# A two-layer fp32 transformer kernel: the MLP's down product as seven block products per quarter, with the result by tokens

## The reference

```python
        h2 = rmsnorm(x, pre_norm_mlp[l])
        y = jnp.square(jax.nn.relu(h2 @ w_up[l])) @ w_down[l]
        x = x + rmsnorm(y, post_norm_mlp[l])
    return x
```

## Time and profile before

| | |
|---|---|
| three runs, median (lowest to highest) | 953.04 us (952.84 to 953.87) |
| profiled execution, its span | 951.7 us |
| TensorE busy, matmuls | 943.3 us, 99%, 5234 records |
| VectorE busy | 587.3 us, 62% |
| ScalarE busy | 417.5 us, 44% |
| GpSimd busy | 100.4 us, 11% |
| DMA | 89 GB/s over the span |

### The profile page before, as it was taken

The page is one execution under the profiler, slowest core; times in us unless marked ns, Lnnn a source line. Parts: engine busy times, 40 slices in busy tenths (PEclk is TensorE's granted clock), DMA queues, the critical chain, the costliest instruction groups (busy, mean ns, idle before and its releaser), DMA issues.

```text
span 951.7 us, 13474 instructions
## 1 busy us (share of the span) xinstructions
PE 943.3 (99%) x5234; PEld 774.8 (81%) x5234; DVE 587.3 (62%) x1062; ACT 417.5 (44%) x773; POOL 100.4 (11%) x109
## 2 busy tenths in 40 slices
PE   9999999999999999999999999999999999999998
PEld 7779777778898777777778889988888888888887
DVE  6668759898658788765656625863244344445545
ACT  6465346455645456444553234562342233212332
POOL 2004204321220000000002212000000000000021
PEclk9999999999999999999999999999999999999999
DMA  7322121122325112121222442353233322323102
GB/s 246 110 69 67 46 67 67 46 67 78 113 70 196 60 64 67 53 72 38 86 67 89 127 161 70 121 187 113 89 108 92 108 89 89 110 89 92 42 1 89
DMA packets 25918, 85.99 MB, mean 90 GB/s; under 512 B 2944, under 2 KB 5952, under 8 KB 25600
## 3 DMA queue, kind: packets, MB, share of 16 engines
q1 hardware_dynamic: 25040, 80.45, 26.1%
q10 hardware_dynamic: 576, 4.36, 1.2%
q0 software_dynamic: 240, 0.33, 0.1%
HBM read 80.93 MB, written 4.19 MB: 89 GB/s over the span
## 4 chain that ended last, share of the span: by engine, by line
PE 86%; DVE 8%; ACT 2%; issue 1%; DMA 1%; SPq 0%; DVEq 0%; ACTq 0%
PE PB L418 13%; PE PB L420 13%; PE PB L419 13%; PE PB L1010 5%; PE PB L1008 5%; PE PB L1009 5%; PE PB L648 4%; PE PB L685 3%; PE PB L663 2%; DVE wl L1504 2%; PE PB L888 2%; PE PB L890 2%; PE PB L889 2%; PE PB L459 2%; PE PB L463 2%; PE PB L458 2%
## 5 line engine op out<-in xcount | busy, mean ns | idle before, releaser
L418 PE MATMUL PB<-hh,wh 128*128 128x512 f32 x576 | 235.2, 408 | 0.0
L420 PE MATMUL PB<-hh,wl 128*128 128x512 f32 x576 | 224.8, 390 | 0.0
L419 PE MATMUL PB<-hl,wh 128*128 128x512 f32 x576 | 224.6, 390 | 0.0
L1504 DVE TENSOR_TENSOR wl<-raw,wh 128x1024 fp32r<-128x1024 f32 (+2 forms) x90 | 113.7, 1263 | 50.9 <-ACT wh L1048 50.5
L418 PEld LDWEIGHTS PB<-hh,wh 128*128 128x128 f32 x576 | 108.2, 188 | 28.2 <-issue 6.4
L420 PEld LDWEIGHTS PB<-hh,wl 128*128 128x128 f32 x576 | 108.1, 188 | 23.3
L419 PEld LDWEIGHTS PB<-hl,wh 128*128 128x128 f32 x576 | 108.3, 188 | 23.0 <-issue 2.2
L1048 ACT ACTIVATE wh<-raw 128x1024 fp32r<-128x1024 f32 (+2 forms) x90 | 91.3, 1018 | 53.4 <-PE PB L463 14.0
L1215 ACT ACTIVATE S<-S,sm 128x256 f32<-128x256 f32 (+3 forms) x96 | 50.6, 528 | 105.0 <-DVE sm L1607 80.8
L1504 DVE TENSOR_TENSOR wl<-AR,wh 128x1024 fp32r<-128x1024 f32 x55 | 67.6, 1230 | 40.4 <-ACT wh L1048 40.4
L1048 ACT ACTIVATE wh<-AR 128x1024 fp32r<-128x1024 f32 x55 | 57.8, 1052 | 71.0 <-PE PB L1010 71.0
(11 more groups left out here) (380 smaller groups left out, 1688.4 us busy)
## 6 DMA issues: line engine op xcount, KB each, us to landing
AR<-in_dne SPq DMA_DIRECT2D x32, 512.0 KB, 3.6
AR<-in_upe SPq DMA_DIRECT2D x24, 512.0 KB, 3.5
raw<-in_w2g SPq DMA_DIRECT2D x16, 512.0 KB, 3.4
raw<-in_w1e SPq DMA_DIRECT2D x10, 512.0 KB, 3.4
raw<-in_w1q SPq DMA_DIRECT2D x8, 512.0 KB, 3.4
raw<-in_woab SPq DMA_DIRECT2D x8, 512.0 KB, 3.5
raw<-in_w2e SPq DMA_DIRECT2D x5, 512.0 KB, 4.5
raw<-in_w1c SPq DMA_DIRECT2D x4, 512.0 KB, 3.4
```

Source lines behind the costliest of these rows:

```text
L418: e.matmul(bank[:], a[:, col(k)], xa[:, k, :], start=k == 0, stop=False)
L419: e.matmul(bank[:], a[:, col(k)], xb[:, k, :], start=False, stop=False)
L420: i = e.matmul(bank[:], b[:, col(k)], xa[:, k, :], start=False, stop=k == 7)
L1504: e.tensor_tensor(low_, raw_of(c), high.bitcast(F32), ALU.subtract).then_inc(*up("lo", c))
```

## The change

The down product of a quarter is (512 tokens x 1024 hidden) by (1024 x 1024). Tokens, hidden and output features are each cut in two, and the eight products of blocks are replaced by seven products of sums and differences of blocks (`PRODUCTS`): four block sums on each side, and the seven results are combined into four. On the hidden side `bh`, `bl` hold high and low of the plain blocks, `th`, `tl` those of four mixed ones (`hidden`, `mixed`). On the weight side slots a, b, c, d hold blocks (two chunks each): `third` writes a - c into c, `second` d - that into d, `fourth` b - that into b, all on VectorE, and a += d is the accumulating DMA that GpSimd issues. A product is two pieces of 12 matmuls. Features are now the stationary operand and weights stream, so results are token by feature, two banks per product, `2 * (n % 3) + s`.

Up tiles only have banks 6 and 7 (`tenant(6 + m % 2, ...)`); banks 4 and 5 are also `TT`, into which VectorE writes the mixed hidden blocks. The products are summed over the quarters in SBUF (`PS`), with the combination folded into the last quarter's sums (`added`). The sum for the second norm is four matmuls of one column (`sums(2, 7)`) ahead of the last product of quarter 0. The result by tokens needs X by tokens: 32 transposes by TensorE (`turned_x`), 16 ahead of the last product and 16 behind it. GpSimd multiplies by the gain, ScalarE squares and sums, VectorE adds the residual (`final`), and the store is by tokens. The tiles by halves of 256 tokens are gone.

```diff
-        s += [("dne", 8 * q + i, NW) for i in range(8)]
+        s += [("dn", 14 * q + i, NW) for i in range(14)]
...
+PRODUCTS = (("b", 0, "a"), ("b", 1, "b"), ("t", 1, "d"), ("t", 0, "a"), ("t", 2, "c"), ("b", 2, "b"), ("t", 3, "d"))
+SUMMED = {2: "s2", 4: "s3", 5: "s4"}
...
+        PS = [[ar(1024 * n + 512 * s, 512) for s in range(2)] for n in range(4)]
+        PS += [[ar(12288 + 1024 * n + 512 * s, 512) for s in range(2)] for n in range(2)] + [[acc[:], R[:]]]
+        SQ2, TT = PS[5], [PB[4], PB[5]]
+        th, tl = (x[:, :, :].rearrange("p (j i) t -> p j (i t)", i=2) for x in (gh, gl))
...
+            def features(n, j, s):
+
+                kind, i = PRODUCTS[n][0:2]
+                w = slice((256 * i + 128 * s), (256 * i + 128 * s) + 128)
+                return (bh[:, j, w], bl[:, j, w]) if kind == "b" else (th[:, j, w], tl[:, j, w])
...
+            def turned_x(b, at):
+
+                for h in range(2):
+                    bank, before = tenant(at + h, "fin", b, h)
+                    e.wait_ge(*to(*before))
+                    for k in range(4):
+                        i = e.transpose(bank[:, col(k)], X[:, 4 * h + k, col(b)], ident)
+                    i.then_inc(*up("xt", b, h))
+
...
+                    bank, before = tenant(6 + m % 2, "re", q, m)
+                    tile(upper(q, m), bank, before, hh, hl)
+                for n in range(7):
+                    got = [tenant(2 * (n % 3) + s, *summed(q, n, s)) for s in range(2)]
+                    if (q, n) == (0, 6):
                         e.wait_ge(*to("xs", 2, 7))
-                        total(2, 6)
-                    half(c, 4, bank, hh, hl)
...
+                        sums(2, 7)
+                    if n == 2:
+                        e.wait_ge(*to("tw", q, 3, 1))
+                    e.wait_ge(*to("lo", piece(q, n, 0)))
+                    if (q, n) == (3, 6):
+                        turned_x(2, 6)
+                        turned_x(3, 2)
+                        e.wait_ge(*to("lo", piece(q, n, 1)))
+                        for s in range(2):
+                            bank, before = got[s]
...
+                            x.then_inc(*up("gemm", "last", s))
+                        turned_x(0, 4)
+                        turned_x(1, 6)
+                        break
+                    for j in range(4):
+                        c = piece(q, n, j // 2)
+                        a, b, w = wh[c % 3], wl[c % 3], slice(512 * (j % 2), 512 * (j % 2) + 512)
+                        if j == 2:
+                            e.wait_ge(*to("lo", c))
+                        if n < 2:
+                            e.wait_ge(*to("bl", q, j, n))
+                        for s in range(2):
+                            bank, before = got[s]
+                            if j == 0:
+                                e.wait_ge(*to(*before))
...
+                            x = e.matmul(bank[:], high, b[:, w], start=False, stop=j == 3)
+                        if j % 2:
+                            x.then_inc(*up("gemm", c))
...
+                    if n == 3:
+                        e.wait_ge(semaphore(f"sum_a{jj}"), 16 * q + 16)
+                    elif n in SUMMED:
+                        e.wait_ge(*to("sc", q, SUMMED[n], jj))
+                    else:
+                        e.wait_ge(*arrived(PRODUCTS[n][2], jj, q, n == 6))
...
-                    e.wait_ge(*to("gemm", c - 3 if c < LAST else CH["upe", 27]))
-                e.activation(wide_high if c == LAST else wh[c % 3][:, 0:PLAN[c][2]], raw_of(c), ACT.Copy).then_inc(*up("hi", c))
+                    e.wait_ge(*to("gemm", c - 3))
+                e.activation(wh[c % 3][:, 0:PLAN[c][2]], raw_of(c), ACT.Copy).then_inc(*up("hi", c))
...
+                e.wait_ge(*to("gemm", upper(q, m)))
...
+                    e.wait_ge(*to("bl", *((q, j - 2) if m > 3 else (q - 1, j + 2)), 1))
+                e.activation(u, seat["re", q, m][:], ACT.Relu).then_inc(*up("re", q, m))
...
+                e.activation(u, u, ACT.Square).then_inc(*up("uq", q, m))
+                e.wait_ge(*to("uq", q, m))
+                if m % 2:
+                    e.activation(bh[:, j, 256:768], u, ACT.Copy).then_inc(*up("uh", q, j, 1))
+                else:
+                    e.activation(bh[:, j, 0:256], u[:, 0:256], ACT.Copy).then_inc(*up("uh", q, j, 0))
...
+            def mixed(q, j):
+
+                e.wait_ge(*to("tc", q, j))
+                for x in range(2):
+                    e.activation(th[:, j, 512 * x:512 * x + 512], TT[x][:], ACT.Copy).then_inc(*up("th", q, j, x))
...
+            def hidden(q, m):
+
+                j, b = m // 2, tmp[m % 4]
+                if m % 2 == 0:
+                    e.wait_ge(*to("uh", q, j, 0))
+                    e.tensor_tensor(bl[:, j, 0:256], b[:, 0:256], bh[:, j, 0:256].bitcast(F32),
+                                    ALU.subtract).then_inc(*up("bl", q, j, 0))
+                    return
+                a, t = tmp[m % 4 - 1], [TT[i // 2][:, 256 * (i % 2):256 * (i % 2) + 256] for i in range(4)]
+                e.wait_ge(*to("uq", q, m))
...
+                e.tensor_tensor(t[0], a[:, 256:512], a[:, 0:256], ALU.subtract).then_inc(*up("tc0", q, j, 0))
+                e.tensor_tensor(t[2], b[:, 256:512], a[:, 256:512], ALU.subtract).then_inc(*up("tc0", q, j, 2))
+                e.wait_ge(*to("tc0", q, j, 0))
+                e.tensor_tensor(t[1], b[:, 256:512], t[0], ALU.subtract).then_inc(*up("tc0", q, j, 1))
+                e.wait_ge(*to("tc0", q, j, 1))
+                e.tensor_tensor(t[3], b[:, 0:256], t[1], ALU.subtract).then_inc(*up("tc", q, j))
+                e.wait_ge(*to("uh", q, j, 1))
+                e.tensor_tensor(bl[:, j, 256:768], b[:], bh[:, j, 256:768].bitcast(F32),
+                                ALU.subtract).then_inc(*up("bl", q, j, 1))
...
+            def mixed(q, j):
+
+                for x in range(2):
+                    t = slice(512 * x, 512 * x + 512)
+                    e.wait_ge(*to("th", q, j, x))
+                    e.tensor_tensor(tl[:, j, t], TT[x][:], th[:, j, t].bitcast(F32), ALU.subtract).then_inc(*up("tw", q, j, x))
...
+                e.tensor_tensor(slot("c", jj), slot("a", jj), slot("c", jj), ALU.subtract).then_inc(*up("sc", q, "s3", jj))
...
+                e.tensor_tensor(slot("d", jj), slot("d", jj), slot("c", jj), ALU.subtract).then_inc(*up("sc", q, "s2", jj))
...
+                e.tensor_tensor(slot("b", jj), slot("b", jj), slot("d", jj), ALU.subtract).then_inc(*up("sc", q, "s4", jj))
...
+                if q < 3:
+                    e.wait_ge(*to(*summed(q - 1, n, s)))
+                    sum_to(PS[n][s], bank, "ye", q, n, s)
+                    return
...
+                if n == 0:
+                    e.wait_ge(*to("yv", 2, 1, s))
+                    sum_to(PS[1][s], bank, "yv", 3, 0, s)
+                    e.wait_ge(*to("yv", 2, 2, s))
+                    sum_to(PS[2][s], bank, "ye", 3, 0, s)
...
+            def final(b, h):
+
+                t = slice(512 * h, 512 * h + 512)
+                e.wait_ge(*(to("yg1") if (b, h) == (1, 1) else to("yg", b, h)))
+                e.wait_ge(*to("tf", b))
+                e.wait_ge(*to("xt", b, h))
+                e.scalar_tensor_tensor(YG[b][:, t], YG[b][:, t], FAC[:, b:b + 1], seat["fin", b, h][:],
+                                       ALU.mult, ALU.add).then_inc(*up("fin", b, h))
...
+                        lo(upper(q, m) + 2)
+                    if q and m < 2:
+                        added(q - 1, 6, m)
+                    if m % 2 == 0 and m > (4 if q == 0 else 0):
+                        mixed(q, m // 2 - 1)
+                    n = m - (4 if q == 0 else 2)
+                    if n in (0, 1):
+                        third(q, n)
...
                     if (q, m) == (1, 1):
                         root(2)
-                    squared(q, m)
...
+                        e.tensor_tensor(acc[:], acc[:], SQ2[k % 2], ALU.add).then_inc(*up("xs", 2, k))
+                    c = CH["dn", 14 * q + n] + 2
+                    if c < len(PLAN):
+                        lo(c)
+                    if n == 1:
+                        mixed(q, 3)
+                    if n in (2, 4):
+                        fourth(q, n // 2 - 1)
+            added(3, 6, 0)
+            for b in (2, 3):
+                for h in (1, 0):
+                    final(b, h)
+            added(3, 6, 1)
+            final(0, 0)
+            final(0, 1)
+            e.wait_ge(*to("ye", 3, 6, 1))
+            e.wait_ge(semaphore("postg"), 16)
+            e.tensor_tensor(YG[1][:, 512:1024], result(1, 1), POSTG[:, 512:1024], ALU.mult).then_inc(*up("yg1"))
+            final(1, 0)
...
-            for m in range(1, 4):
-                added_y(3, m)
-            for x in range(2):
-                t = half_of[x]
-                for m in (4, 5, 6, 7)[:4 - x]:
-                    e.wait_ge(*to("yq", 3, m, x))
```

(41 more changed lines are left out.)

423 lines of the change are left out of this document (200 added, 223 removed), and 14 rows, old and new, of the table SIGNALS.

## The result

The changed kernel takes **945.67 us** in the median of four runs (944.15 to 947.49), the kernel before 952.96 (952.84 to 953.87): a ratio of 0.9922, 95% interval 0.9908 to 0.9936. It is faster, by 7.3 us, where 16.7 were forecast; the range of 930.5 to 944.5 misses it by 1.2. Run again on another chip it took 944.9 (ratio 0.9911, interval 0.9896 to 0.9926).

The account below looks back on a forecast made before the run. TensorE, busy 99% of the span, was taken as the bound: 951.7 - 23.5 + 1.9 + 1.9 + 4.3 + 0.3 + 0.8 + 0.4 - 2.8 = 935.0 us of span, 936.3 with 1.3 for the median; range 930.5 to 944.5.

Parts of the forecast that it names:

- tiles by halves gone: Down product: its last four tiles' 192 half-width matmuls, with one matmul of ones among them, go from TensorE, -23.5 us.
- 16 transposes ahead of the last product: TensorE: 16 of the 32 transposes of X come before the last product, about 0.115 us each, +1.9 us.
- waits at (0,6) and (1,1): Up tiles: (0,6) waits for the Relu of (0,4), +1.9 us; (1,1) waits for root(2) to free bank 7, +4.3.
- restart, and half clock behind three waits: TensorE behind the two up-tile waits: a restart of a step or so, +0.3 us; no half clock in the sum.
- VectorE late in the last down stage, GpSimd beside it: Last down stage: VectorE's 35.3 us against TensorE's 34.5, +0.8; two GpSimd gain products slowing VectorE by 0.25 each, +0.4.
- sum in bank 7, small steps: TensorE: the second norm's sum becomes four one-column matmuls instead of two records of 512 columns, cost 0.
- the end: After the last wide matmul: eleven VectorE instructions, then a store of 2.65 us; 7.1 us instead of 9.9, -2.8.
- the rival on the clock: TensorE's granted clock falls to its lower level behind the 4.3 us wait: 938 to 942 us, chance 0.05.
- VectorE bounds the last quarter: Last quarter: VectorE's instructions 10% dearer, adding 3 to 4 us there and 1 elsewhere: 939.5 to 944.5 us, chance 0.17.
- The first 672 matmuls of the down product: Down stage: seven products, 672 matmuls over four quarters, cost as before although features are loaded and weights stream, 0.
- The accumulating DMA was covered: Each quarter: slot a += slot d takes 8.4 us, at most 15.5, with 15 to 19.6 us of cover, cost 0.
- The rivals that let it decide: Accumulating DMA outlasts its cover, so piece 6's high part waits: 944 to 951 us, chance 0.03; slower than 953, 0.06.

Follow-up runs that it names:

- The kernel before with the wait alone: The kernel before with its ones matmul total(2) moved to the bank that up tile (1,1) takes, so that tile waits for root(2): 960.19 us against 953.18.
- the four banks: The changed kernel with up tiles taking banks 6, 7, 2 and 3 in turn instead of 6 and 7 alone: 936.68 us, ratio 0.9824.
- the late gain: The changed kernel with GpSimd's products with the gain started only behind VectorE's last low part: 940.39 us, ratio 0.9862.
- with root(2) first: The changed kernel with root(2) on VectorE ahead of the low parts of tiles (1,3) and (1,0), bank 7 still shared: 938.24 us, ratio 0.9842.
- the kernel with the weight sum on VectorE: The changed kernel with slot a += slot d made by VectorE instead of GpSimd's accumulating DMA: 944.95 us, ratio 0.9909.
- unedited: The changed kernel run again without any edit, as the measure for the experiments on the other chip: 944.9 us, ratio 0.9911.
- the last four kernels: The changed kernel with four banks and late gain products (932.28 us); also quarter 0's second weight sum later (931.03); that with a += d on VectorE (933.3), or last store split (930.84).

## Why the prediction was wrong, point by point

The direction, the places and most sizes held; the sum failed by 9.4 us, for two of its terms and two smaller ones. In the profiles' spans, the forecast's terms, and what the profile after shows:

| term | forecast | measured |
|---|---|---|
| tiles by halves gone | -23.5 | -23.5 |
| 16 transposes ahead of the last product | +1.9 | +2.0 |
| waits at (0,6) and (1,1) | +6.2 | 1.8 + 4.2, with their gaps +6.3 |
| restart, and half clock behind three waits | +0.3 | +0.3 and +4.8 |
| VectorE late in the last down stage, GpSimd beside it | +1.2 | 0.8 + 0.7 + 2.2 = +3.7 |
| sum in bank 7, small steps | 0 | +0.9 |
| the end | -2.8 | -1.9 |
| opening of this one profile | 0 | +1.8 |
| sum (span 951.7) | 935.0 | 946.2 (rows add to 946.1) |

**The failed step is the clock.** The forecast put 0.3 behind the two waits and made the fall of the clock a rival of 0.05, though it had found the wait of 4.2 that sets it off, and had seen that nothing in the kernel before could speak for a full clock behind such a wait, since its longest was 1.1. The Trainium skill ("TensorE: Matmul & The Clock Gate", "HAM oscillation — how this bites in real kernels") says that kernels whose TensorE idles for a few us pay with a throttled stretch; the trace agrees, for 4.2 us, and shows the same behind waits of 1.8 and 2.2, shorter than the 3 to 5 of the page's example. That the trace before showed no such fall was no evidence against it. The kernel before with the wait alone, and the four banks, settle the cause from both sides: 7.0 us for a wait of 4.6, and 8.2 off the median (10.1 off the profiled span, where the third stretch stayed away too) where waits of 6.0 went and one of 1.1 came. By itself this step would have made the forecast 941.1, inside the 938 to 942 of the rival on the clock; it took the next one and the small rows of the table to leave the range.

**The second is GpSimd beside VectorE.** The text read 0.25 us per product off one pair of rows and took it for the price. There GpSimd's instruction (909.09, 1.30 us) ended 0.4 us after VectorE's began (909.99). So the two overlapped for 0.4 us only, and VectorE's record ended 1.08 behind GpSimd's, as the low parts of the new stage do. In the new stage overlaps of 0.79, 1.24, 1.23 and 1.20 us cost VectorE 0.65, 1.09, 1.10 and 1.07: in all five places the loss is the overlap less some 0.15. The small price was that of a short overlap. The rule of the Trainium skill ("SBUF — State Buffer", "Who interferes with whom"), that the two block each other for a whole instruction, was weighed and set aside for that row, which is no evidence against it. The page also says that a VectorE instruction with one SBUF input at most is left alone (outside its two-port modes), and the sums from PSUM agree (675 to 692 ns). The trace after bears the rule out (3.9 us on VectorE, 2.5 of them on TensorE), and the late gain shows that this was the cause. The rival "VectorE bounds the last quarter" had the right engine, with a price of 10% on all its instructions; the price was on four of them.

**The end.** Eleven instructions in a row, as worked out, but a final took 0.66, not 0.605, and the last store, of 256 KB where the row's was of 128, 3.15 to the end, not 2.65: 0.9.

**What held.** The first 672 matmuls of the down product cost as before, with features loaded instead of weights. Both waits were found from the order, with chains that were right: moving root(2) first one, then two places took off 1.8 and then the rest. The accumulating DMA was covered; its estimate of 8.4 us was nearly twice the 4.5 measured, with a cover of 15, so that nothing hung on it. The rivals that let it decide had no part.

**What stays open.** The same wait is not always followed by the slow stretch. Behind the 1.8 us at (0,6) the clock fell in six of the seven profiles that have this wait (it did not with root(2) first), behind the 2.2 in front of the last product in three of five, behind 4.2 and 4.6 in all six; it fell behind the 1.8 in the last stage of the kernel with the weight sum on VectorE, and not behind the 2.4. The runs of one kernel differ by 1 to 3 us while such waits are in it (943.86 to 945.89 unedited) and by 0.6 to 0.8 in the last four kernels without them (930.38 to 931.16 in one). That fits, but shows little: the kernel before has no such wait, and its nine runs beside one of these experiments differ by 1.4. What decides it was not tried. Of the 0.9 in the row of the sum in bank 7 and small steps, some 0.5 is that sum: its four matmuls left eight records and took 1.04 us, like the row of eight records, where the two records before took 0.45, so the forecast's 0 for it was some 0.5 us too small. The rest was not followed up.

## What to carry to other kernels

A new wait of a few us on a TensorE that never paused before should be priced as the wait and, in most cases, a half-clock stretch of some 3.4 us behind it (16 of the 20 waits of 1.8 to 4.6 us here; 1.6 us each, 2.6 for the longest), and looked for in short windows, since a page in slices of 24 us shows a full clock. Work moved to GpSimd is not free for VectorE when both read SBUF: where VectorE sets the pace, four products cost it more on GpSimd than on itself. And when one small instruction lets a bank go, list everything ahead of it on its engine and what each of these waits for; other banks for the up tiles were worth 8.2 us here, an earlier place for that instruction 6.7, without touching the arithmetic.

## What the hardware showed that was not expected

- A slow stretch costs only where TensorE sets the pace: in the kernel with the weight sum on VectorE it fell into a part that VectorE bounded, which took just the 2.3 us of VectorE's added work longer and nothing for the stretch.
- A DMA that adds one SBUF slot of 512 KB to another landed in 4.5 us (at most 6.5), against 3.4 to 4.2 in the median for plain loads of the same size behind the opening.
- GpSimd is slowed too: its product of 512 columns took 1.64 to 1.75 us beside VectorE's instructions of two SBUF inputs and 1.26 to 1.30 beside others or alone.
- The same 256 KB store at the end took from 2.3 to 3.2 us to the end of the span, across these kernels, for a reason that stays open, and cutting it in two changed nothing.
